# Two gated MLPs: second products by Strassen's scheme on token halves, with weight sums on GpSimd

## The chip, the cores and the metric

One core of a Trainium2 chip runs the whole program. The metric is the device time of one execution in microseconds, the median of the runs shown. The engines are TensorE (PE; its weight loads are listed apart as PEld), VectorE (DVE), ScalarE (ACT), GpSimd (POOL) and SyncE (SP), which issues most DMAs.

## The reference, cut to what matters

Batch 1, 512 tokens, width 1024, all in float32. Five other stages lie around two gated MLPs (an S5 mixer, two attention stages, a Mamba-2 layer and norms). The change touches only the MLPs, with 2816 hidden channels:

```
def conv_ffn(xn, w_up, conv_w, conv_b, w_down):
    val, gate = jnp.split(xn @ w_up, 2, axis=-1)
    gp = jnp.pad(gate, ((0, 0), (CONV_W - 1, 0), (0, 0)))
    gc = conv_b + conv_w[0] * gp[:, 0:seq]
    for j in range(1, CONV_W):
        gc = gc + conv_w[j] * gp[:, j:j + seq]
    return (jax.nn.silu(gc) * val) @ w_down
...
h = h + conv_ffn(rms_norm(h, ffn_norm[layer]), ffn_w_up[layer], ...)
```

`xn @ w_up` is the first product, `(...) @ w_down` the second one.

## The kernel before, in words

Channels lie on the 128 partitions, the 512 tokens on the free axis. The state `K.h` is 8 tiles of 128x512; the hidden activations of an MLP are 22 tiles. Every dense product is made in three passes of reduced-precision matmuls: weight and activation are each split into a high part (rounded to fp32r) and the remainder, and high*high, high*low and low*high are added up in one PSUM bank (`product`, lines 431, 432, 434). The remainder times remainder is dropped.

Weights come from device memory in *units*, in the order of one list (`weight_units`). A unit of an MLP's first product is 8 blocks of 128 columns (1024 columns of float32, 512 KB). An output of the second product sums over 11 hidden tiles in each half of the MLP, cut into a unit of 6 blocks and one of 5. For each unit SP issues a load into one of 5 buffers `raw` (`weight_loads`), ACT rounds it into one of 3 buffers `wh` (`split_hi`, line 391), DVE subtracts and writes `wl` (`split_lo`, line 402), and PE counts the unit as done. So the high part of unit n waits until PE is done with unit n-3, and the load of unit n+5 waits for both parts of unit n. ACT and DVE execute in the order of the code: `split_hi(K, act, upto)` and `split_lo(K, dve, upto)` are placed between the other work, two units (`LA`) ahead of PE.

`ffn_pe`, `ffn_act`, `ffn_dve` and `ffn_pool` are one MLP. A half is an *up* stretch, then a *down* stretch. In an up stretch PE makes for each hidden tile f the gate and the value (two units, 48 matmuls of 512 columns). For each f DVE multiplies the gate with the norm's factors (line 705), makes the convolution (802, 805, 808) and one `wl`, waits for ACT's SiLU (771), multiplies by the norm (812) and the value (815); ACT rounds the result into `fh` (776), DVE writes the remainder `fl` (819), and then makes the other `wl`. In a down stretch PE makes the 8 output tiles, and DVE adds each to `h` (719). In the second half ACT and DVE also make the next stage's input from each finished `h` tile (`norm_act`: 542, 562; `norm_dve`: 550), and GpSimd sums the squares (577). GpSimd has nothing else to do in the MLPs.

Of the kernel before, what the change touches and what calls it, by code (L numbers as in the profile page):

```python
# [8 lines left out]
P = 128  # L9
# [4 lines left out]
HALF = NF // 2  # L14
# [16 lines left out]
RAW, NH, LA = 5, 3, 2  # L31

# [211 lines left out]
def weight_units():  # L244

    u = []

    def tile(name, m, k0=0, k1=8):
        for a, z in pieces(k0, k1):
            u.append((name, "T", m, a, z))  # L250

    def tiles(name, ms):
        for m in ms:
            tile(name, m)

    def values(name):
        for half in range(2):
            for k in range(0, 8, 2):
                u.append((name, "N", D + half * 512, k, k + 2))

    def ffn(i):
        tiles(f"up{i}", (NF, 0))
        for half in range(2):
            for f in range(half * HALF, (half + 1) * HALF):
                if f:
                    tiles(f"up{i}", (NF + f, f))
            for m in range(8):
                tile(f"down{i}", m, half * HALF, (half + 1) * HALF)
# [34 lines left out]
WIDTH = {"T": P, "N": 512, "N32": 32}  # L303
# [3 lines left out]
OFFS = [P * sum(COLS[:n]) for n in range(len(UNITS) + 1)]  # L307


def done(name, m, k0=0, k1=8):  # L310

    return UNIT[(name, "T", m, pieces(k0, k1)[-1][0])] + 1

# [20 lines left out]
    + ["gcp", "conv", "silu", "gv", "fh", "fl"]  # L334
# [6 lines left out]
    + ["lam", "lama", "akc", "aqc", "ag", "agg", "agt", "asp", "asc", "aex", "acm", "atp", "akp", "amix"]  # L341
# [399 lines left out]
def ffn_pe(K, pe, layer):  # L741
# [15 lines left out]


def ffn_act(K, act, layer):
# [4 lines left out]
    for half in range(2):  # L764
        for f in range(half * HALF, (half + 1) * HALF):
# [5 lines left out]
            act.e.activation(t[:, :], t[:, :], ACT.Silu).then_inc(K.S["silu"], 1)  # L771
# [5 lines left out]
        for m in range(8):  # L777
            split_hi(K, act, done(down, m, half * HALF, (half + 1) * HALF) + LA)
            if half:
                norm_act(K, act, b + 1, m)  # L780


def ffn_dve(K, dve, layer):
# [8 lines left out]
    for half in range(2):  # L792
        for f in range(half * HALF, (half + 1) * HALF):
# [17 lines left out]
            dve.wait_ge("silu", i + 1)  # L811
# [2040 lines left out]
def combine2_dve(K, dve, n):  # L2852
# [3 lines left out]
    dve.wait_ge("lam", 4)  # L2856
# [169 lines left out]
def att2_dve(K, dve):  # L3026
# [197 lines left out]
def att1_tensors(K, sb):  # L3224
# [11 lines left out]
    K.sp = [[(sb("sph0", [P, 1024], R32), sb("spl0", [P, 1024], R32)), (K.wh[0], K.wl[0])],  # L3236
# [56 lines left out]
def build_program(nc, d):  # L3293
    with ExitStack() as ctx:
# [18 lines left out]
        K.xs = [sb(f"xs{i}", [P, T]) for i in range(2)]  # L3313
# [126 lines left out]
def _weights(inputs):  # L3440
# [8 lines left out]
    for n, (name, kind, m, k0, k1) in enumerate(UNITS):  # L3449
        c0, cw = (m * P, P) if kind == "T" else (m, WIDTH[kind])  # L3450
# [26 lines left out]
```

## Time and profile before

| | us |
|---|---|
| time, median of 3 runs (1982.88 to 1983.55) | 1983.34 |
| span of the profiled execution, first to last instruction | 1981.3 |
| what lies around the span (1983.34 - 1981.3) | 2.0 |
| PE busy in the span | 1953.9 |
| DVE, ACT, POOL busy | 1329.3, 900.1, 243.7 |
| first MLP: up 258.4 to 367.3, down to 427.1, up to 546.8, down to 606.6 | 348 |
| second MLP: up 895.1 to 1003.9, down to 1063.8, up to 1183.4, down to 1243.2 | 348 |

The execution that was profiled has no time of its own beside its span; the span and the median differ by 2.0 us. A span entry for PE counts overlapping matmuls once. The columns of each view are explained at its first group of rows below.

### The profile page before, as it was taken

The numbers are of one execution on the slowest core, as the hardware profiler recorded it, in microseconds if no ns is written. First come the engines' busy times: TensorE is split into PE (matmuls) and PEld (weight loads), VectorE is DVE, ScalarE is ACT, GpSimd is POOL, SyncE is SP. The second block draws the span as 40 slices with busy tenths as digits, with TensorE's granted clock in tenths as the row PEclk, the third lists the DMA queues.
The fourth block names the chain that finished last, engine by engine and source line by source line (L and its number), as shares of the span: only waits on it lengthen the run. The fifth ranks groups of instructions, "written<-read, shape, count | busy, mean of one in ns | idle before, by whom it ended". The sixth has DMA issues, their size and how long they took to land.

```text
span 1981.3 us, 25092 instructions
## 1 busy us (share of the span) xinstructions
PE 1953.9 (99%) x9474; PEld 1562.3 (79%) x9474; DVE 1329.3 (67%) x1907; ACT 900.1 (45%) x1483; POOL 243.7 (12%) x237
## 2 busy tenths in 40 slices
PE   9999999999999999999999999999999999999998
PEld 7777888888888776788888888788888888886666
DVE  8995476446644449747644664778787778437985
ACT  5674332223233348733222223565555545236774
POOL 4131100000010000010000001133333332000002
PEclk9999999999999999999999999999999999999998
DMA  8465322232233220022223223222222223322112
GB/s 290 113 144 155 106 83 92 88 121 91 81 105 106 86 96 11 1 90 91 93 88 117 96 77 107 86 64 70 86 75 80 85 65 107 96 75 75 38 38 75
DMA packets 81367, 180.44 MB, mean 91 GB/s; under 512 B 17888, under 2 KB 33632, under 8 KB 81248
## 3 DMA queue, kind: packets, MB, share of 16 engines
q1 hardware_dynamic: 77680, 172.08, 27.9%
q0 software_dynamic: 3424, 6.23, 1.1%
q8 instruction: 76, 1.25, 0.3%
q10 hardware_dynamic: 144, 0.52, 0.1%
q14 instruction: 43, 0.35, 0.1%
HBM read 171.53 MB, written 7.27 MB: 90 GB/s over the span
## 4 chain that ended last, share of the span: by engine, by line
PE 85%; DVE 8%; ACT 3%; issue 2%; DMA 1%; SPq 1%; POOLq 0%; POOL 0%; DVEq 0%; ACTq 0%
PE psum L431 20%; PE psum L434 20%; PE psum L432 20%; PE psum L472 2%; PE psum L473 2%; PE psum L475 2%; PE psum L453 2%; PE psum L899 1%; PE psum L901 1%; PE psum L900 1%; PE psum L1781 1%; PE psum L456 1%; PE psum L454 1%; PE psum L2824 1%; DVE wl L402 1%
## 5 line engine op out<-in xcount | busy, mean ns | idle before, releaser
L402 DVE TENSOR_TENSOR wl<-raw,wh 128x1024 fp32r<-128x1024 f32 (+3 forms) x337 | 381.4, 1133 | 303.6 <-ACT wh L391 302.9
L431 PE MATMUL psum<-xh,wh 128*128 128x512 f32 x1376 | 543.9, 395 | 1.7 <-DVE xl L550 1.7
L434 PE MATMUL psum<-xh,wl 128*128 128x512 f32 x1376 | 537.0, 390 | 1.6 <-DVE wl L402 1.6
L432 PE MATMUL psum<-xl,wh 128*128 128x512 f32 x1376 | 536.4, 390 | 0.0
L391 ACT ACTIVATE wh<-raw 128x1024 fp32r<-128x1024 f32 (+3 forms) x337 | 316.0, 939 | 294.8 <-PE psum L434 198.1
L431 PEld LDWEIGHTS psum<-xh,wh 128*128 128x128 f32 x1376 | 258.6, 188 | 61.9 <-issue 2.9
L434 PEld LDWEIGHTS psum<-xh,wl 128*128 128x128 f32 x1376 | 258.7, 188 | 57.9 <-DVE wl L402 3.7
L432 PEld LDWEIGHTS psum<-xl,wh 128*128 128x128 f32 x1376 | 258.8, 188 | 55.1 <-issue 2.4
L577 POOL TENSOR_TENSOR rs<-rs,sq 128x512 f32<-128x512 f32 x35 | 46.6, 1331 | 1088.8 <-ACT sq L562 1088.8
L434 PE MATMUL psum<-fh,wl 128*128 128x512 f32 x352 | 136.9, 389 | 0.0
L432 PE MATMUL psum<-fl,wh 128*128 128x512 f32 x352 | 136.9, 389 | 0.0
L431 PE MATMUL psum<-fh,wh 128*128 128x512 f32 x352 | 136.9, 389 | 0.0
L719 DVE TENSOR_TENSOR h<-h,psum 128x512 f32<-128x512 f32 x87 | 59.3, 684 | 67.7 <-PE psum L434 65.4
L431 PEld LDWEIGHTS psum<-fh,wh 128*128 128x128 f32 x352 | 66.1, 188 | 13.8
L434 PEld LDWEIGHTS psum<-fh,wl 128*128 128x128 f32 x352 | 66.1, 188 | 13.7
L432 PEld LDWEIGHTS psum<-fl,wh 128*128 128x128 f32 x352 | 66.1, 188 | 13.6
L542 ACT ACTIVATE xh<-h,par 128x512 fp32r<-128x512 f32 x64 | 43.5, 715 | 63.8 <-DVE h L719 55.2
L771 ACT ACTIVATE ny<-ny 128x512 f32<-128x512 f32 x22 | 13.9, 632 | 109.6 <-DVE ny L808 109.6
L771 ACT ACTIVATE nv<-nv 128x512 f32<-128x512 f32 x22 | 13.9, 632 | 104.0 <-DVE nv L808 104.0
L472 PE MATMUL psum<-xh,wh 128*128 128x512 f32 x152 | 59.6, 392 | 0.4 <-ACT xh L1382 0.4
L475 PE MATMUL psum<-xh,wl 128*128 128x512 f32 x152 | 59.2, 390 | 0.0
L473 PE MATMUL psum<-xl,wh 128*128 128x512 f32 x152 | 59.2, 390 | 0.0
(526 smaller groups left out, 3339.1 us busy)
## 6 DMA issues: line engine op xcount, KB each, us to landing
raw<-d_w SPq DMA_DIRECT2D x224, 512.0 KB, 3.5
raw<-d_w SPq DMA_DIRECT2D x32, 384.0 KB, 3.0
raw<-d_w SPq DMA_DIRECT2D x48, 256.0 KB, 2.6
raw<-d_w SPq DMA_DIRECT2D x32, 320.0 KB, 2.9
Mt<-d_kd SPq DMA_DIRECT2D x64, 64.0 KB, 2.4
bc<-d_bc SPq DMA_DIRECT2D x8, 256.0 KB, 5.3
d_ud<-ust SPq DMA_DIRECT2D x8, 256.0 KB, 3.1
U<-d_ud POOLq DMA_DIRECT2D x64, 32.0 KB, 2.4
```

The costliest lines, as they stand in the source:

```text
L391: act.e.activation(K.wh[n % NH][:, 0:COLS[n]], K.raw[n % RAW][:, 0:COLS[n]], ACT.Copy).then_inc(K.S["hi"], 1)
L402: dve.e.tensor_tensor(K.wl[n % NH][:, 0:COLS[n]], K.raw[n % RAW][:, 0:COLS[n]], K.wh[n % NH][:, 0:COLS[n]].bitcast(F32), ALU.subtract).the ...
L431: pe.e.matmul(b[:, :], WH[:, o:o + P], XH, start=(k == k0), stop=False)
L432: pe.e.matmul(b[:, :], WH[:, o:o + P], XL, start=False, stop=False)
L434: mm = pe.e.matmul(b[:, :], WL[:, o:o + P], XH, start=False, stop=(k == k1 - 1))
L453: pe.e.matmul(b[:, :], WH[:, o:o + P], XH, start=(k == 0), stop=False)
L472: pe.e.matmul(b[:, :], WH[:, o:o + P], XH, start=(k == 0), stop=False)
L473: pe.e.matmul(b[:, :], WH[:, o:o + P], XL, start=False, stop=False)
L475: mm = pe.e.matmul(b[:, :], WL[:, o:o + P], XH, start=False, stop=(k == 7))
L542: act.e.activation(K.xh[:, k, :], K.h[:, k, :], ACT.Copy, scale=K.par(gain, k)).then_inc(K.S["xh"], 1)
L577: pool.e.tensor_tensor(K.acc[:, :], K.acc[:, :], K.sq[k % 2][:, :], ALU.add).then_inc(K.S["acc"], 1)
L719: dve.e.tensor_tensor(K.h[:, m, :], K.h[:, m, :], K.bank[bank][:, :], ALU.add).then_inc(K.S[signal], 1)
```

## The change

The second product now takes hidden tiles in pairs (k, k+1), outputs in pairs q and tokens in halves L and R of 256. In such a 2x2 by 2x2 product the weights are the blocks A11, A12, A21, A22 and the activations B11, B12 (first hidden tile, L and R), B21, B22. Strassen's scheme in Winograd's form makes it with seven products of 256 columns instead of eight. It needs four sums of the weights (S1 to S4) and four of the activations (T1 to T4), and recombines the products.

- The MLP is cut into 12 and 10 hidden tiles instead of 11 and 11 (`SPANS`). In the first half all 8 outputs go by the scheme (4 pairs), in the second 6 outputs (3 pairs); outputs 6 and 7 of the second half are made by `product` as before.
- A unit "S" holds 4 blocks for one pair of outputs and one of hidden tiles: 256 KB are loaded, GpSimd appends three more blocks of sums (`weight_sums`), and ACT and DVE split the 7 blocks, 896 columns. `split_hi` waits for GpSimd's count `wsum`.
- PE makes 7 x 3 matmuls of 256 columns for a unit, into four banks (`seven_products`).
- For an odd hidden tile, DVE makes T2, T3, T4 and the remainders of 512 and of 1024 columns; for an even one T1 and a remainder of 256 (first half) or 512 columns (`hidden_dve`). T1 to T4 lie in `K.T`, named `xs` in the rows.
- A pair of outputs is added to `h` by eight instructions of DVE and a copy of one product out of PSUM by ACT (`seven_to_h`).
- GpSimd makes all weight sums of an MLP before it adds the first squares (`ffn_pool`). The spare buffers that the first attention borrows, and the counts of a few semaphores, are renamed.

```diff
-HALF = NF // 2
+SPANS = ((0, 12), (12, NF))
+DOWN_PAIRS = (4, 3)
...
+def weight_sums(K, pool, name):
+    for n, u in enumerate(UNITS):
+        if u[:2] != (name, "S"):
+            continue
...
+        pool.wait_ge(f"raw{n % RAW}", 16 * (n // RAW + 1))
+        pool.e.tensor_tensor(s13.rearrange("p (n c) -> p n c", n=2), a21.unsqueeze(1).broadcast_to([P, 2, P]),
+                             others.rearrange("p (n c) -> p n c", n=2), ALU.add).then_inc(K.S["pool"], pool.up())
+        pool.wait_ge("pool", pool.n)
+        pool.e.tensor_tensor(s2, s1, a11, ALU.add).then_inc(K.S["pool"], pool.up())
+        pool.wait_ge("pool", pool.n)
+        pool.e.tensor_tensor(s4, s2, a12, ALU.add).then_inc(K.S["wsum"], 1)
...
+A22, A11, A12, S1, S3, S2, S4 = range(7)
+SEVEN = ((A11, "B11", 0, 0), (A12, "B21", 2, 0), (S4, "B22", 2, 1), (A22, "T4", 3, 0), (S1, "T1", 3, 1), (S2, "T2", 0, 1),
+         (S3, "T3", 1, 0))
+def seven_products(K, pe, name, q, banks, x, freed, k0, k1):
...
+    for k in range(k0, k1, 2):
+        n, WH, WL = next_unit(K, pe, name, "S", q, k)
+        pe.wait_ge("hi", n + 1)
...
+            pe.e.matmul(out, WH[:, o:o + P], XH, start=first, stop=False, skip_group_check=True)
+            pe.e.matmul(out, WH[:, o:o + P], XL, start=False, stop=False, skip_group_check=True)
+            pe.wait_ge("lo", n + 1)
+            mm = pe.e.matmul(out, WL[:, o:o + P], XH, start=False, stop=(k == k1 - 2), skip_group_check=True)
+        mm.then_inc(K.S["unit"], 1)
...
+def seven_to_h(K, dve, q, banks, end, copy, before, signal):
...
+    split_lo(K, dve, end + 1 + LA)
+    dve.wait_ge(*before)
+    dve.wait_ge("unit", end)
+    a = add(h1, h1, p23[:, :], ALU.add)
+    dve.wait_ge("fa", copy)
+    u = add(U, p16[:, R], p1, ALU.subtract)
+    dve.wait_ge("dve", a)
+    add(h1[:, L], h1[:, L], p1, ALU.add)
+    dve.wait_ge("dve", u)
+    w = add(Q, U, p7[:, L], ALU.subtract)
+    split_lo(K, dve, end + 2 + LA)
+    b = add(h1[:, R], h1[:, R], U, ALU.subtract)
+    c = add(h2, h2, p45[:, :], ALU.add)
+    dve.wait_ge("dve", b)
+    e.tensor_tensor(h1[:, R], h1[:, R], p45[:, R], ALU.subtract).then_inc(K.S[signal], 1)
+    dve.wait_ge("dve", max(w, c))
+    two = h2.rearrange("p (n c) -> p n c", n=2)
+    e.tensor_tensor(two, two, Q.unsqueeze(1).broadcast_to([P, 2, 256]), ALU.add).then_inc(K.S[signal], 1)
...
             split_hi(K, act, v + 1 + LA)
-            if f >= 13:
-                act.wait_ge("unit", done(down, 7, 0, HALF))
-            act.wait_ge("gv", i + 1)
-            act.e.activation(K.fh[layer][:, f % 13, :], t[:, :], ACT.Copy).then_inc(K.S["fh"], 1)
...
+            act.wait_ge("gv", val_read(i))
+            if f % 2 == 0:
+                n = 1 + half
+                act.e.activation(hidden(K.fh[layer], half, f, "B11", n), t[:, 0:256 * n], ACT.Copy).then_inc(K.S["fh"], 1)
+            else:
+                act.e.activation(hidden(K.fh[layer], half, f, "B21", 2), t[:, :], ACT.Copy).then_inc(K.S["fh"], 1)
+                act.wait_ge("gv", val_read(i) + 1)
+                act.e.activation(hidden(K.fh[layer], half, f, "T1", 4), K.T[:, :], ACT.Copy).then_inc(K.S["fh"], 1)
...
 def ffn_pool(K, pool, layer):
+    weight_sums(K, pool, f"down{layer}")
     add_squares(K, pool, 2 + 2 * layer)
```

The order of DVE's instructions at the end of the first up stretch of the first MLP (the last hidden tile, then the first units of the second product). Before, with the last tile's gate at the top (`psum,rs`), `wl` of 768 and 640 columns for the second product, and `h<-h,psum` for the first output:

```order
L705 TENSOR_TENSOR fg_1<-psum,rs 128x512
L802 TENSOR_SCALAR nv<-fg_1,par 128x512
L805 SCALAR_TENSOR_TENSOR nv<-fg_1,par,nv 128x511
L808 SCALAR_TENSOR_TENSOR nv<-fg_1,par,nv 128x510
L402 TENSOR_TENSOR wl<-raw,wh 128x640
L812 TENSOR_TENSOR nv<-nv,rs 128x512
L815 TENSOR_TENSOR nv<-nv,psum 128x512
L819 TENSOR_TENSOR fl<-nv,fh 128x512
L402 TENSOR_TENSOR wl<-raw,wh 128x768
L402 TENSOR_TENSOR wl<-raw,wh 128x640
L719 TENSOR_TENSOR h<-h,psum 128x512
```

And now, from the convolution's last instruction of hidden tile 11 (an odd one) to the first pair of outputs; `xs` is `K.T`:

```order
L990 SCALAR_TENSOR_TENSOR ny<-fg_2,par,ny 128x510
L418 TENSOR_TENSOR wl<-raw,wh 128x896
L994 TENSOR_TENSOR ny<-ny,rs 128x512
L997 TENSOR_TENSOR ny<-ny,psum 128x512
L955 TENSOR_TENSOR xs<-ny,xs 128x256
L956 TENSOR_TENSOR xs<-ny,nv 128x256
L958 TENSOR_TENSOR xs<-ny,xs 128x256
L961 TENSOR_TENSOR fl<-ny,fh 128x512
L961 TENSOR_TENSOR fl<-xs,fh 128x1024
L418 TENSOR_TENSOR wl<-raw,wh 128x896 x7
L475 TENSOR_TENSOR h<-h,psum 128x512
```

Between the last multiplication by the value and the next `wl` there are now five instructions of DVE instead of one.

ACT's order around the end of the first pair of outputs in the second half, now (`wh<-raw` are the splits, `xs<-psum` the copy of one product, `xh`, `rs` and `sq` the next stage's input and its squares):

```order
L406 ACTIVATE wh<-raw 128x896 x6
L927 ACTIVATE xs<-psum 128x256
L406 ACTIVATE wh<-raw 128x896
L633 ACTIVATE xh<-h,par 128x512
L650 ACTIVATE rs<-h 128x512
L633 ACTIVATE xh<-h,par 128x512
L653 ACTIVATE sq<-h 128x512
L406 ACTIVATE wh<-raw 128x896 x4
```

Two `h` tiles become ready together, so four activations stand between two splits, where before there were two for every two splits.

## Rows read from the trace of the kernel before

**Rows 1.** The page: span, and each engine's busy time and share.

```profile
span 1981.3 us, 25092 instructions
...
PE 1953.9 (99%) x9474; PEld 1562.3 (79%) x9474; DVE 1329.3 (67%) x1907; ACT 900.1 (45%) x1483; POOL 243.7 (12%) x237
```

**Rows 2.** Windows of MLP 1, second to fourth stretch: us, busy (instructions), clock, DMA.

```profile
367.30:427.10 59.80, 59.80 (x265) 49.53 (x264) 21.54 (x26) 13.77 (x17) 0.00 (x0) 1.00 0.36 113
427.10:546.80 119.70, 119.70 (x530) 99.12 (x529) 77.14 (x98) 33.75 (x43) 0.00 (x0) 1.00 0.28 89
546.80:606.60 59.80, 59.80 (x265) 49.55 (x264) 28.07 (x32) 21.69 (x31) 7.77 (x6) 1.00 0.36 113
```

**Rows 3.** Timeline, PE in attention 1: start, duration, line, tiles.

```profile
753.30 0.28 PE L1064 MATMUL psum<-spl,tri 128*128 128x256 f32 x1
...
753.77 0.40 PE L1069 MATMUL psum<-sph,tri 128*128 128x512 f32 x1
```

**Rows 4.** The same, 12 us later.

```profile
765.18 0.28 PE L1064 MATMUL psum<-spl,tri 128*128 128x256 f32 x1
...
765.54 0.28 PE L1068 MATMUL psum<-wh,tri 128*128 128x256 f32 x1
```

**Rows 5.** Timeline, DVE, a hidden tile of the up stretch.

```profile
351.22 0.69 DVE L705 TENSOR_TENSOR fg<-psum,rs 128x512 f32<-128x512 f32 x1 [0.96 <-PE psum L434]
...
353.31 0.75 DVE L808 SCALAR_TENSOR_TENSOR ny<-fg,par,ny 128x510 f32<-128x510 f32 x1
355.71 1.23 DVE L402 TENSOR_TENSOR wl<-raw,wh 128x1024 fp32r<-128x1024 f32 x1 [1.65 <-ACT wh L391]
...
357.58 0.69 DVE L815 TENSOR_TENSOR ny<-ny,psum 128x512 f32<-128x512 f32 x1
358.96 0.69 DVE L819 TENSOR_TENSOR fl<-ny,fh 128x512 fp32r<-128x512 f32 x1 [0.70 <-ACT fh L776]
```

**Rows 6.** Timeline, ACT, the same tile: SiLU and rounding into fh.

```profile
354.10 0.63 ACT L771 ACTIVATE ny<-ny 128x512 f32<-128x512 f32 x1 [5.10 <-DVE ny L808]
...
358.30 0.63 ACT L776 ACTIVATE fh<-ny 128x512 fp32r<-128x512 f32 x1 [2.62 <-DVE ny L815]
```

**Rows 7.** Timeline, DVE, gate of hidden tile 1 of MLP 1.

```profile
269.31 0.68 DVE L705 TENSOR_TENSOR fg<-psum,rs 128x512 f32<-128x512 f32 x1
```

**Rows 8.** Timeline, PE: the first weights' remainder that came late.

```profile
275.07 0.50 PE L434 MATMUL psum<-xh,wl 128*128 128x512 f32 x1 [0.46 <-DVE wl L402]
```

**Rows 9.** Groups by form, DVE: count, busy us, mean ns, idle before.

```profile
L1713 DVE TENSOR_TENSOR mst<-mst,sq 128x256 f32<-128x256 f32 x16 | 6.8, 425 | 15.6 <-ACT mst L1705 15.3
```

**Rows 10.** The same, ACT.

```profile
L391 ACT ACTIVATE wh<-raw 128x1024 fp32r<-128x1024 f32 x224 | 235.2, 1052 | 152.4 <-PE psum L434 58.0 <-PE psum L901 50.0 <-PE psum L475 36.1
...
L391 ACT ACTIVATE wh<-raw 128x256 fp32r<-128x256 f32 x1 | 0.4, 417 | 0.0
```

**Rows 11.** The same, POOL.

```profile
L577 POOL TENSOR_TENSOR rs<-rs,sq 128x512 f32<-128x512 f32 x35 | 46.6, 1331 | 1088.8 <-ACT sq L562 1088.8
...
L2244 POOL TENSOR_TENSOR s5small<-s5small 128x64 f32<-128x64 f32 x1 | 0.3, 328 | 0.1
```

**Rows 12.** Timeline, POOL, second down stretch of MLP 1.

```profile
571.54 1.29 POOL L577 TENSOR_TENSOR rs<-rs,sq 128x512 f32<-128x512 f32 x1 [6.18 <-ACT sq L562]
```

**Rows 13.** Timeline, DVE, the same place.

```profile
572.23 1.42 DVE L402 TENSOR_TENSOR wl<-raw,wh 128x768 fp32r<-128x768 f32 x1 [1.39 <-ACT wh L391]
...
576.98 0.69 DVE L719 TENSOR_TENSOR h<-h,psum 128x512 f32<-128x512 f32 x1 [1.81 <-PE psum L434]
```

**Rows 14.** Timeline, DVE, first down stretch: a remainder of 768 columns.

```profile
369.86 0.96 DVE L402 TENSOR_TENSOR wl<-raw,wh 128x768 fp32r<-128x768 f32 x1
```

**Rows 15.** Timeline, ACT, second down stretch: the next stage's input.

```profile
577.70 0.72 ACT L542 ACTIVATE xh<-h,par 128x512 fp32r<-128x512 f32 x1 [3.39 <-DVE h L719]
578.33 0.62 ACT L562 ACTIVATE sq<-h 128x512 f32<-128x512 f32 x1
```

**Rows 16.** DMA issues: count, KB each, median us to landing.

```profile
raw<-d_w SPq DMA_DIRECT2D x48, 256.0 KB, 2.6
```

More of the change, by code:

```diff
@@ L262, in ffn @@
         tiles(f"up{i}", (NF, 0))
-        for half in range(2):
-            for f in range(half * HALF, (half + 1) * HALF):
+        for half, (f0, f1) in enumerate(SPANS):
+            for f in range(f0, f1):
                 if f:
                     tiles(f"up{i}", (NF + f, f))
-            for m in range(8):
-                tile(f"down{i}", m, half * HALF, (half + 1) * HALF)
+            for q in range(DOWN_PAIRS[half]):
+                for k in range(f0, f1, 2):
+                    u.append((f"down{i}", "S", q, k, k + 2))
+            for m in range(2 * DOWN_PAIRS[half], 8):
+                tile(f"down{i}", m, f0, f1)
     tiles("a_w_in", range(8))
@@ L307, with pair_done @@
 OFFS = [P * sum(COLS[:n]) for n in range(len(UNITS) + 1)]
+SUMS = [sum(u[1] == "S" for u in UNITS[:n + 1]) for n in range(len(UNITS))]
+SPLIT = [(P, 7 * P) if u[1] == "S" else (0, c) for u, c in zip(UNITS, COLS)]
 def done(name, m, k0=0, k1=8):
     return UNIT[(name, "T", m, pieces(k0, k1)[-1][0])] + 1
+def pair_done(name, q, k1):
+    return UNIT[(name, "S", q, k1 - 2)] + 1
 SEMS = (
@@ L763, in ffn_act @@
     rsqrt_first(K, act, b)
-    for half in range(2):
-        for f in range(half * HALF, (half + 1) * HALF):
+    for half, (f0, f1) in enumerate(SPANS):
+        for f in range(f0, f1):
             i = layer * NF + f
@@ L770, in ffn_act @@
             act.other("silu")
[L771 removed]
+            act.e.activation(t[:, :], t[:, :], ACT.Silu).then_inc(K.S["fa"], 1)
             split_hi(K, act, v + 1 + LA)
[L773 to L780 removed]
+            if half:
+                act.wait_ge("unit", pair_done(down, 3, SPANS[0][1]))
@@ new lines, in ffn_act @@
+        for q in range(DOWN_PAIRS[half]):
+            for k in range(f0, f1, 2):
+                split_hi(K, act, UNIT[(down, "S", q, k)] + 1 + LA)
+            end = pair_done(down, q, f1)
+            split_hi(K, act, end + 1 + LA)
+            act.wait_ge("unit", end)
+            act.wait_ge("fl", 33 * layer + 3 * (f1 // 2))
+            if q:
+                act.wait_ge("h" if half else "hpart", (8 + 16 * layer if half else 8 * layer) + 2 * q)
+            act.e.activation(K.T[:, 512:768], K.bank[DOWN_BANKS[half][q % 2][0]][:, 0:256], ACT.Copy).then_inc(K.S["fa"], 1)
+            split_hi(K, act, end + 2 + LA)
+            if half:
+                norm_act(K, act, b + 1, 2 * q)
+                norm_act(K, act, b + 1, 2 * q + 1)
@@ new lines, in ffn_act, with hidden_dve @@
+        for m in range(2 * DOWN_PAIRS[half], 8):
+            split_hi(K, act, done(down, m, f0, f1) + LA)
+            norm_act(K, act, b + 1, m)
+def hidden_dve(K, dve, layer, half, f):
+    i, e = layer * NF + f, dve.e
+    t, before, g = K.gg[i % 2], K.gg[(i + 1) % 2], 33 * layer + 3 * (f // 2)
+    L, R = slice(0, 256), slice(256, 512)
+    T1, T2, T3, T4 = (K.T[:, 256 * n:256 * n + 256] for n in range(4))
+    if half:
+        dve.wait_ge("unit", pair_done(f"down{layer}", 3, SPANS[0][1]))
+    dve.wait_ge("gv", val_read(i))
+    if f % 2 == 0:
+        n = 1 + half
+        dve.wait_ge("fl", g)
+        own(K, dve, "dve", e.tensor_tensor(T1, t[:, R], t[:, L], ALU.subtract))
+        dve.wait_ge("fh", g + 1)
+        e.tensor_tensor(hidden(K.fl[layer], half, f, "B11", n), t[:, 0:256 * n],
+                        hidden(K.fh[layer], half, f, "B11", n).bitcast(F32), ALU.subtract).then_inc(K.S["fl"], 1)
+        return
+    e.tensor_tensor(T2, t[:, R], T1, ALU.subtract).then_inc(K.S["dve"], dve.up())
+    e.tensor_tensor(T3, t[:, R], before[:, R], ALU.subtract).then_inc(K.S["dve"], dve.up())
+    dve.wait_ge("dve", dve.n)
+    e.tensor_tensor(T4, t[:, L], T2, ALU.subtract).then_inc(K.S["gv"], 1)
+    for first, n, count, src in (("B21", 2, g + 2, t[:, :]), ("T1", 4, g + 3, K.T[:, :])):
+        dve.wait_ge("fh", count)
+        e.tensor_tensor(hidden(K.fl[layer], half, f, first, n), src, hidden(K.fh[layer], half, f, first, n).bitcast(F32),
+                        ALU.subtract).then_inc(K.S["fl"], 1)
@@ L791, in ffn_dve @@
     newton(K, dve, K.ny[:, :], K.nv[:, :], K.ns[:, :], K.rs[:, :]).then_inc(K.S["rs"], 1)
-    for half in range(2):
-        for f in range(half * HALF, (half + 1) * HALF):
+    for half, (f0, f1) in enumerate(SPANS):
+        for f in range(f0, f1):
             i = layer * NF + f
```

142 lines of the change are left out of this document (98 added, 44 removed).

## The prediction

> **What bounds the kernel now.** I read the page first: PE is busy for 1953.9 of 1981.3 us, DVE for 67%, ACT for 45%, GpSimd for 12% [rows 1]. Then the windows of the first MLP. In the down stretches PE has no gap (59.80 busy of 59.80), DVE is busy for 21.5 or 28 us, ACT for 14 or 22, at a granted clock of 1.00 [rows 2]. So matmul time saved here is saved on the path, as long as DVE and ACT, which prepare every operand, stay ahead. The up stretches have less room than their shares say: a hidden tile gives PE 48 matmuls, and DVE and ACT work on it in turns, each waiting for the other. Therefore I then read the timeline of one such tile, tile by tile.
>
> **PE: what is removed and added.** A down stretch has 8 x 11 x 3 = 264 matmuls of 512 columns in 59.80 us, 0.2265 us each [rows 2]. One MLP has 528, 119.6 us. After: 4 pairs of outputs x 6 pairs of hidden tiles + 3 x 5 = 39 units of 21 matmuls, 819 of 256 columns, and 2 x 10 x 3 = 60 of 512. The nearest rows for 256 columns with a new weight tile each are those of attention 1: four starts in 753.77 - 753.30 = 0.47 us, 0.117 each [rows 3], and three in 0.36 us, 0.120 each [rows 4]. I take 0.119: 819 x 0.119 + 60 x 0.2265 = 97.5 + 13.6 = 111.1 us, 8.5 less for an MLP, 17.1 for both. At 0.120 it is 15.4, at 0.117 it is 20.4. Against the one eighth of the work that is dropped, some is lost since 256 columns take more than half the time of 512.
>
> The Trainium skill (TensorE: Matmul & The Clock Gate, "Back-to-back issue gap") gives N/2.4 + 2.5 ns at full clock, 216 ns for 512 columns and 109 for 256. By that an MLP would save 528 x 0.216 - 819 x 0.109 - 60 x 0.216 = 11.8 us, both 23.7. The rows (226.5 and 117 to 120) do not agree, and they decide.
>
> **The up stretch.** In the rows of one tile, from the start of L705: L808 2.09, ACT's SiLU 2.88, the first remainder L402 4.49, L815 6.36, ACT's fh 7.08, fl 7.74 [rows 5, 6]. fh is followed by ACT's split of 1.05 us [rows 10] and the second remainder of 1.23; the next L705 could start at 9.83. PE takes 48 x 0.2268 = 10.89 us, so before DVE gains 1.06 us for each tile when it is behind. Now an odd tile goes: L815 ends at 7.05, three instructions of 256 columns (0.425 each [rows 9], the first two overlapped by 0.09) to 8.27, ACT rounds 1024 columns to 9.36, DVE's remainder ends at 10.62, the second wl at 11.75, next L705 at 11.66. For an even tile the 256-column rounding (0.417 [rows 10]) gives 9.62 in the first half, and 512 columns 9.83 in the second. A pair takes 21.28 or 21.49 of PE's 21.77 us. PE isn't delayed in the stretch itself (a remainder has some 4.5 us to spare), but a lag of DVE is hardly made good any more.
>
> The lag at the start is known: L705 of tile 1 comes at 269.31 [rows 7]; 19 units of 5.44 us back from 367.3 [rows 2], less 0.5 for a wait of PE, put the end of its gate at 263.4, so that it is 5.8 us late; it costs PE about 0.5 us in tile 2 [rows 8]. Now it starts at about 5.3 (tile 0 has smaller roundings), PE loses about the same, and it falls by 0.49 a pair from 4.0 at tile 3 to 1.85 at tile 11 (0.24 of it since the units there have 896 columns). The second up stretch starts with DVE 4.0 us late, because `seven_to_h` of the last pair holds DVE until 9.8 us after PE's start, where the wait is for a unit of 5.44 us; but there tile 12 misses its first wl and SiLU's split, 2.1 us, so that the lag is 0.9 at tile 13 and about 0 at the end.
>
> **From up to down.** Let PE begin the first S unit at V. It takes two units, 2 x 21 x 0.119 = 5.0 us, and needs the remainder of the third at V + 5.24. A wl of 896 columns takes (0.96 + 1.23)/2 = 1.09 us [rows 14, 5], ACT's split 0.93 [rows 10]. DVE reaches L815 at V + 0.95 + lag and, by the steps above, ends that remainder 5.26 later: V + 6.2 + lag. Before, a unit had 3.4 or 4.1 us of PE and only one fl, and nothing was late. So PE now waits 1.0 us + lag: 2.85 us in the first half, 1.0 in the second, before GpSimd is counted.
>
> **GpSimd.** 128x512 took 1.29 us undisturbed [rows 12], 128x64 0.33 [rows 11], so 2.15 ns a column: 0.74 us for 256 columns, 0.46 for each 128, 1.67 and two short waits for a unit, below PE's 2.50. A unit's load lands 2.6 us after its issue [rows 16], which follows the wl five units ahead; the sums are ready some 5 us before ACT needs them. But GpSimd and DVE exclude each other: the addition from 571.54 to 572.83 made the remainder that started at 572.23 last 1.42 us instead of 0.96 [rows 12 to 14], that is until 0.82 us after GpSimd was through, as if it had started just before that end. Instructions that read PSUM, such as L719, are not stretched. GpSimd's hold of a unit is at most 1.67 - 3 x 0.14 = 1.24 us. I laid the seven sums that fall into tiles 8 to 11 (each lands 2.7 us after a wl) against DVE's steps. Every second one falls into the wait for SiLU and costs nothing; the others push DVE by 0.54, 0.27, 0.24 and 0.27. That is 1.3 us in the first half, and 0.5 in the second, where the lag's reserve takes the rest. Bounds: none, and 7 x 1.24 = 8.7 us for a transition. I take the sums' values, since they rest on the same steps. PE waits 4.2 and 1.5 us, 5.7 for an MLP.
>
> The Trainium skill (GPSIMD Engine Reference, "Specifications" and "Engine selection") says that GpSimd shares its SBUF port with VectorE, with contention where a DVE instruction has two SBUF inputs, and that elementwise work belongs on VectorE, about twice as fast. The trace agrees on the contention (1.42 against 0.96 us) and with 1.29 against 0.69 us. This rule speaks against the change; its result is the second rival below.
>
> **End of a pair of outputs.** After PE's last matmul of a pair ACT splits (0.93) and copies, and DVE does wl, four additions, wl, four additions. The eight cost 3 x 0.69 [rows 13] + 5 x 0.425 = 4.2 us, against 2 x 0.69 before. In the first half the wl after them ends at 8 us after the pair, and PE wants it at 4 x 2.50 + 0.24 = 10.24: no wait. In the second half ACT waits for h at 6.1 and makes xh, sq, xh, sq (0.72, 0.62 [rows 15]) to 8.6; its split ends at 9.4, DVE's wl at 10.55: PE waits 0.35 us. For the second pair GpSimd's sum of squares (1.29) lies before the wl, which ends at 11.45: 1.25 us. The third pair is followed by units of 3.4 us and hides it. Queued behind ACT's wait for h are all splits. 1.6 us for an MLP. Nothing changes after output 7.
>
> **The sum.** Profiled span 1981.3 + 2.0 around it = 1983.3, the median. 1983.3 - 17.1 + 2 x (5.7 + 1.6) = 1983.3 - 17.1 + 14.6 = 1980.8 us.
>
> **Rivals.**
> First, DVE's lag disappears: the sums all fall into waits and the first up stretch ends without lag. For it speaks that PE waits for a remainder only at tile 2 before, and that half of DVE's steps are waits for ACT; against it the 0.49 us a pair, which cannot repay 4 us. PE would wait 1.0 at each transition and 0.35 twice: 2.7 for an MLP. 1983.3 - 17.1 + 5.4 = 1971.6.
> Second, and slower: GpSimd's hold decides at the transitions. Three separate additions with waits between them may each catch a DVE instruction; with half the full hold, 0.62 us a unit, seven units push DVE by 4.3 instead of 1.3 and, in the second half, 3.5 instead of 0.5. That adds 3.0 us at four transitions, 12: 1992.8. It decides from (1987.3 - 1980.8)/4 = 1.6 us more at a transition, 0.4 us a unit in the mean. For it: DVE wants the port for half of a tile's time. Against: a wait for ACT after every second step lets it catch up.
> Third, 256-column matmuls are bound by their weight loads at 0.120 or a little more in a long row, with every PE number else as above: 0.123 would take 6.6 us of the gain, 1987.4. Rows 3 and 4 are short rows of four, which speaks for a doubt; their starts stay at 0.12, which speaks against.
>
> **How the numbers follow.** The forecast's case has 0.42, the first rival 0.24, the second 0.24, the third 0.10. A measurement of this kernel tells about 0.2% (4 us) from no change, so faster is below 1979.4, slower above 1987.3. The forecast's own range, with transitions off by 1 us each, is 1976 to 1986: 0.15 of its 0.42 is faster, 0.26 same, 0.01 slower. The first rival is faster. The second is slower but for 0.02. The third is same or slower in equal parts. Sum: faster 0.39, same 0.33, slower 0.28. The range reaches from 1969 (first rival, with 0.117 for a matmul) to 1995 (second rival, somewhat beyond its mean); outside lies a tenth on either side.
>
> **What would show it.** Starts 0.119 apart in the units of 256 columns and down stretches near 24 x 2.50 + 4.2 = 64 us (first half) and 15 x 2.50 + 13.6 + 1.5 + 1.6 = 54 us (second). A wait of PE for wl in the third S unit of each down stretch, about 4 and 1.5 us, and small ones in the fifth unit of pairs 1 and 2 in the second half; none in the first half's pairs. L705 of tile 11 about 3 us behind its gate, and of tile 21 under 1. Additions of GpSimd of 0.46 to 0.74 us, longer where they meet DVE. I am wrong in the mechanism if PE waits elsewhere, such as for ACT's high part or for `wsum`, or if the up stretches grow by more than 1 us each.

## The result and the profile after

The changed kernel takes 1994.13 us (median of 4 runs, 1993.26 to 1995.15), the kernel before on the same chip 1983.44 (1982.88 to 1984.29): a ratio of 1.0053 [1.0038, 1.0067]. It is slower by half a per cent; the forecast was 1980.8. The page of the profiled execution, for [rows 1]:

```profile
span 1992.5 us, 27125 instructions
...
PE 1946.9 (98%) x10176; PEld 1587.2 (80%) x10176; DVE 1465.0 (74%) x2123; ACT 952.9 (48%) x1541; POOL 438.9 (22%) x471
```

The span grew by 11.2 us, and PE's busy time fell by 7.0, so PE stands still for 18.2 us more (what lies between its records). DVE is busy for 136 us more, GpSimd for 195. Which stretches changed is read from windows: us, busy (instructions) of PE, PEld, DVE, ACT, POOL, then the granted clock, DMA share and GB/s. The first three lines are the stretches of the first MLP that [rows 2] show of before, the next two the down stretches of the second MLP; the last is a piece of the first line.

```profile
378.12:445.85 67.73, 63.95 (x505) 63.16 (x504) 47.56 (x58) 26.75 (x31) 45.52 (x57) 0.95 0.38 115
445.85:554.68 108.83, 108.83 (x483) 90.09 (x481) 83.26 (x116) 35.45 (x44) 13.19 (x18) 1.00 0.28 85
554.68:612.58 57.90, 52.76 (x377) 49.37 (x375) 45.02 (x58) 27.21 (x39) 33.03 (x34) 1.00 0.37 110
1021.37:1087.91 66.54, 62.72 (x505) 62.11 (x504) 46.87 (x58) 26.76 (x31) 47.13 (x57) 0.97 0.39 117
1196.74:1254.79 58.05, 52.81 (x377) 49.38 (x375) 45.03 (x58) 27.39 (x39) 33.24 (x34) 1.00 0.35 103
...
388.10:393.60 5.50, 5.50 (x26) 5.50 (x27) 2.21 (x3) 0.95 (x1) 2.79 (x6) 0.50 0.46 143
```

The up stretch is unchanged: its window now holds ten tiles, 10.88 us each, as PE's 48 x 0.2268. The four down stretches took 59.8 us each; now they sum to 250.2 instead of 239.2. That is all but 0.2 us of the loss. In two of them the clock is below 1.00, where [rows 2] have 1.00.

PE, in the steady part of a down stretch (start, duration, line, tiles), for [rows 3, 4]:

```profile
400.01 0.28 PE L462 MATMUL psum<-fh,wl 128*128 128x256 f32 x1
400.13 0.28 PE L459 MATMUL psum<-fh,wh 128*128 128x256 f32 x1
```

Starts lie 0.120 apart. The Trainium skill (TensorE: Matmul & The Clock Gate, "Back-to-back issue gap") has a formula for an isolated matmul that gives 0.109; this trace does not agree.

The second S unit of the first down stretch (its wait is at 381.89) and the third one (386.39 and 388.07), PE:

```profile
381.89 0.39 PE L462 MATMUL psum<-fh,wl 128*128 128x256 f32 x1 [0.62 <-DVE wl L418]
...
386.39 0.38 PE L459 MATMUL psum<-fh,wh 128*128 128x256 f32 x1 [1.97 <-ACT wh L406]
386.61 0.28 PE L460 MATMUL psum<-fl,wh 128*128 128x256 f32 x1
388.07 0.58 PE L462 MATMUL psum<-fh,wl 128*128 128x256 f32 x1 [1.18 <-DVE wl L418]
388.45 0.42 PE L459 MATMUL psum<-fh,wh 128*128 128x256 f32 x1
388.67 0.41 PE L460 MATMUL psum<-fl,wh 128*128 128x256 f32 x1
```

PE waits three times in 6.2 us, and behind the last wait the starts go from 0.12 to 0.21 apart: TensorE is at 1.2 instead of 2.4 GHz (0.50 in the window 388.10 to 393.60). It had stood still for 2.0 and 1.2 us just before. 25 matmuls here and 16 in the second MLP start 0.213 apart, 41 x 0.093 = 3.8 us. What DVE and ACT did meanwhile, for [rows 5 to 7]:

```profile
374.86 1.58 DVE L418 TENSOR_TENSOR wl<-raw,wh 128x896 fp32r<-128x896 f32 x1 [0.34 <-ACT wh L406]
376.37 0.68 DVE L796 TENSOR_TENSOR fg<-psum,rs 128x512 f32<-128x512 f32 x1
...
380.74 1.09 DVE L418 TENSOR_TENSOR wl<-raw,wh 128x896 fp32r<-128x896 f32 x1 [1.54 <-ACT wh L406]
...
383.98 0.43 DVE L958 TENSOR_TENSOR xs<-ny,xs 128x256 f32<-128x256 f32 x1
...
386.67 3.61 DVE L418 TENSOR_TENSOR wl<-raw,wh 128x896 fp32r<-128x896 f32 x3
```

```profile
384.44 1.06 ACT L917 ACTIVATE fh<-xs 128x1024 fp32r<-128x1024 f32 x1 [0.62 <-DVE xs L958]
385.40 2.61 ACT L406 ACTIVATE wh<-raw 128x896 fp32r<-128x896 f32 x3
```

The third S unit's high part is the first of the three at 385.40. It stands behind the rounding of T1 to T4 on ACT, which waits for T4 (L958). Its remainder, the first of three from 386.67, is what PE waits for until 388.07. And the last gate of the stretch (L796) was itself late. The additions of GpSimd around it, for [rows 12]:

```profile
374.76 0.73 POOL L431 TENSOR_TENSOR raw<-raw 128x256 f32<-128x256 f32 x1 [1.63 <-DMA raw<-d_w]
375.58 1.19 POOL L434 TENSOR_TENSOR raw<-raw 128x128 f32<-128x128 f32 x1
376.84 0.46 POOL L436 TENSOR_TENSOR raw<-raw 128x128 f32<-128x128 f32 x1
```

The remainder from 374.86 took 1.58 us where 1.09 is usual (380.74), and GpSimd's addition of 128 columns beside it 1.19 where 0.46 is usual (376.84). Each held the other up: the addition of 256 columns that was under way until 375.49 held up the remainder, and the remainder held up the next addition. Lastly PE's waits grouped (engine, line, what it waited for, us in total, times, longest):

```profile
PE psum L462 <- DVE wl L418: 11.8, 10, 1.7
PE psum L459 <- ACT wh L406: 6.2, 6, 2.0
```

By stretch, measured by what they add to a down stretch without waits (60.47 and 51.42 us, from the last experiment but one) and without the clock's share: the first down stretches wait 5.0 and 4.6 us, the second ones 6.5 and 6.6, of which 2.4 and 2.5 lie at their start and 4.1 and 4.1 behind pairs 1 and 2. The account of the 11.2 us: matmuls -15.4, waits +22.7, clock +3.8, in all 11.1. The 22.7 are more than the 18.2 us of standing still because a wait adds more than the gap between two records: the record before it lasts 0.28 us where the next start would have come after 0.12, and the first start behind it is followed by the next after 0.22 (386.39 to 386.61).

### The profile page after: what moved, and what is told of

It reads as the page before. It is cut to its first block, busy times and chain, and to the rows that moved or that the text cites. A ratio compares the mean times of both kernels' runs of the same rounds, so it can differ in the third digit from the quotient of the medians.

```text
span 1992.5 us, 27125 instructions
## 1 busy us (share of the span) xinstructions
PE 1946.9 (98%) x10176; PEld 1587.2 (80%) x10176; DVE 1465.0 (74%) x2123; ACT 952.9 (48%) x1541; POOL 438.9 (22%) x471
## 4 chain that ended last, share of the span: by engine, by line
PE 63%; DVE 21%; ACT 8%; issue 7%; DMA 1%; SPq 0%; DVEq 0%; ACTq 0%
PE psum L522 10%; PE psum L525 10%; PE psum L523 10%; ACT wh L406 4%; DVE wl L418 3%; PE psum L462 3%; PE psum L459 3%; PE psum L460 3%; PE psum L563 2%; PE psum L566 2%; PE psum L564 2%; PE psum L544 1%; PE psum L1084 1%; PE psum L1085 1%; PE psum L1086 1%
## 5 line engine op out<-in xcount | busy, mean ns | idle before, releaser
L418 DVE TENSOR_TENSOR wl<-raw,wh 128x1024 fp32r<-128x1024 f32 (+3 forms) x359 | 427.9, 1197 | 280.0 <-ACT wh L406 279.4
L525 PE MATMUL psum<-xh,wl 128*128 128x512 f32 x1376 | 537.6, 391 | 1.7 <-DVE wl L418 1.7
L523 PE MATMUL psum<-xl,wh 128*128 128x512 f32 x1376 | 536.3, 390 | 0.0
L431 POOL TENSOR_TENSOR raw<-raw 128x256 f32<-128x256 f32 x78 | 71.1, 911 | 468.6 <-DMA raw<-d_w 468.5
L462 PE MATMUL psum<-fh,wl 128*128 128x256 f32 x546 | 157.4, 288 | 11.8 <-DVE wl L418 11.8
L459 PE MATMUL psum<-fh,wh 128*128 128x256 f32 x546 | 157.2, 288 | 6.2 <-ACT wh L406 6.2
L460 PE MATMUL psum<-fl,wh 128*128 128x256 f32 x546 | 156.1, 286 | 0.0
L462 PEld LDWEIGHTS psum<-fh,wl 128*128 128x128 f32 x546 | 106.6, 195 | 13.8 <-DVE wl L418 13.8
L459 PEld LDWEIGHTS psum<-fh,wh 128*128 128x128 f32 x546 | 106.7, 195 | 7.8 <-ACT wh L406 7.6
L434 POOL TENSOR_TENSOR raw<-raw 128x128 f32<-128x128 f32 x78 | 62.9, 806 | 6.1
L436 POOL TENSOR_TENSOR raw<-raw 128x128 f32<-128x128 f32 x78 | 58.9, 755 | 6.1
```

Source lines behind the costliest of these rows:

```text
L418: dve.e.tensor_tensor(K.wl[n % NH][:, 0:w], K.raw[n % RAW][:, o:o + w], K.wh[n % NH][:, 0:w].bitcast(F32), ALU.subtract).then_inc(K.S["lo" ...
L431: pool.e.tensor_tensor(s13.rearrange("p (n c) -> p n c", n=2), a21.unsqueeze(1).broadcast_to([P, 2, P]), others.rearrange("p (n c) -> p n ...
L434: pool.e.tensor_tensor(s2, s1, a11, ALU.add).then_inc(K.S["pool"], pool.up())
L436: pool.e.tensor_tensor(s4, s2, a12, ALU.add).then_inc(K.S["wsum"], 1)
L459: pe.e.matmul(out, WH[:, o:o + P], XH, start=first, stop=False, skip_group_check=True)
L460: pe.e.matmul(out, WH[:, o:o + P], XL, start=False, stop=False, skip_group_check=True)
```

## The experiments

Theory A, the prediction's with larger sizes: the splits of the next units queue behind the serial chain of the last hidden tile and behind the pair's additions; GpSimd's hold of the port lengthens that chain; the clock falls when PE has waited. B: GpSimd's additions are the whole cause. C: they hardly matter. The kernel before took 1983.39 us beside the first four and 1983.19 beside the last four. Lines with < are taken out of the changed kernel, those with > put in.

**No sums.** GpSimd's additions are left out, so the weights' products use unsummed blocks.

```diff
<         if UNITS[n][1] == "S":
<             act.wait_ge("wsum", SUMS[n])
...
<     weight_sums(K, pool, f"down{layer}")
```

> GpSimd's weight sums are left out (ACT and DVE split whatever lies in the three blocks of the sums), so nothing shares the SBUF port with DVE in the MLPs but the sums of squares. Theory A (the waits come from the chain that DVE and ACT walk in turns, now longer by T1 to T4, by the eight instructions for a pair and by the splits queued behind them; GpSimd only lengthens it): PE's waits in the two MLPs fall from 22.5 to about 9 to 11 us, the clock stays up (another 4), 1976 to 1980 us. Theory B (GpSimd's hold on the port is what makes DVE late): hardly a wait is left, 1967 to 1970 us. Theory C (port contention matters little): within 4 us of 1994.

Measured 1982.59 us (10 runs), ratio 0.9996 [0.9986, 1.0005]: 11.5 less than with the sums. A's number is missed by some 3 us, B's by 13, and C's (no more than 4 us) is excluded. Windows:

```profile
378.20:443.13 64.93, 62.48 (x505) 62.07 (x504) 41.41 (x56) 26.30 (x31) 0.00 (x0) 0.97 0.42 119
551.96:606.78 54.82, 52.19 (x376) 49.23 (x375) 40.53 (x58) 27.35 (x38) 9.75 (x6) 1.00 0.38 116
1015.62:1079.06 63.44, 60.98 (x505) 60.57 (x504) 41.41 (x56) 26.32 (x31) 0.00 (x0) 1.00 0.42 123
```

```profile
374.88 0.68 DVE L793 TENSOR_TENSOR fg<-psum,rs 128x512 f32<-128x512 f32 x1
```

Without the weight sums the first down stretch still waits 3.0 us, by the chain alone, and the second 3.4, with GpSimd's sums of squares still beside it (9.75 us in its window). The gate of tile 11 comes 3.32 us before the stretch, with the sums 1.75. The clock fell once (0.97, 15 matmuls), in the first MLP; the second MLP's first down stretch has waits of the same size and stayed at 1.00. So the sums cost some 9.7 us of waits and 2.5 of clock, more than twice what had been counted, and they aren't the whole cause.

**No T.** T1 to T4, their rounding and remainder are cut to 8 columns; PE reads blocks of the plain hidden tile in their place.

```diff
>         block = {"T1": "B11", "T2": "B21", "T3": "B22", "T4": "B11"}.get(block, block)
...
<     T1, T2, T3, T4 = (K.T[:, 256 * n:256 * n + 256] for n in range(4))
---
>     T1, T2, T3, T4 = (K.T[:, 256 * n:256 * n + 8] for n in range(4))
```

> T1 to T4 and their splits are cut to 8 columns, and PE multiplies B blocks in their place; all counts, waits and matmuls stay. Theory A: DVE has no lag at the end of the up stretches, the waits at the first units of the second product (4.9 and 2.4 us for an MLP) and the fallen clock go, those at the ends of pairs stay: 1976 to 1979 us. Theory B: the port is held as before, so at least half of the waits at the first units stay, 1984 to 1990 us.

Measured 1976.67 (5 runs), 0.9966 [0.9953, 0.9979]: what A had, and far from B's.

```profile
377.41:437.99 60.58, 60.58 (x505) 60.52 (x504) 44.91 (x56) 24.45 (x29) 45.90 (x54) 1.00 0.43 128
546.82:602.54 55.72, 52.44 (x377) 49.31 (x375) 43.33 (x58) 26.28 (x38) 32.23 (x33) 1.00 0.38 114
```

With the sums in place and the tile's chain shorter no wait is left at the start of a down stretch, and the clock stays at 1.00. Only the waits behind pairs remain, 4.3 us in the second stretch. The hold alone makes nothing late at the start of a down stretch.

**Plain addition.** A pair is added with two instructions of 512 columns, so h isn't the combination wanted.

```diff
<     u = add(U, p16[:, R], p1, ALU.subtract)
...
<     add(h1[:, L], h1[:, L], p1, ALU.add)
...
<     w = add(Q, U, p7[:, L], ALU.subtract)
>     e.tensor_tensor(h1, h1, p23[:, :], ALU.add).then_inc(K.S[signal], 1)
...
>     e.tensor_tensor(h2, h2, p45[:, :], ALU.add).then_inc(K.S[signal], 1)
```

> A pair of outputs is added to h by two instructions of 512 columns instead of eight (six are left out; ACT's copy stays). Theory A: the waits at the ends of pairs in the second half (4.2 us for an MLP) go and nothing else changes: 1985 to 1987 us. Theory B: GpSimd's additions before the late wl stay, so 1 to 2 us of each MLP's 4.2 stay: 1988 to 1990 us.

Measured 1986.14 (10 runs), 1.0013 [1.0003, 1.0022], 8.0 less than the changed kernel, as A had it.

```profile
553.98:607.28 53.30, 51.94 (x377) 49.17 (x376) 37.48 (x40) 27.48 (x38) 31.17 (x33) 1.00 0.40 119
```

The waits behind the pairs are gone, those at the start (1.9 us here, 6.4 with the clock in the first stretch) aren't. To leave six of a pair's eight additions out is thus enough to remove the 8.2 us that stood there, with the weight sums in place. That it is also possible without leaving anything out is shown by the run "Pair early" below.

**Units early.** In the last tile of each up stretch the third and fourth S units are split before the norm's multiplication, the fifth before ACT rounds T1 to T4.

```diff
>             if f == f1 - 1:
>                 split_hi(K, act, v + 5)
...
>     if f == SPANS[half][1] - 1:
>         split_lo(K, dve, done(f"up{layer}", NF + f) + 6)
...
<             split_lo(K, dve, done(up, NF + f) + 1 + LA)
---
>             split_lo(K, dve, done(up, NF + f) + 1 + LA + 2 * (f == f1 - 1))
```

> Nothing is left out; in the last hidden tile of each up stretch ACT and DVE split the third and fourth unit of the second product right after the second, before the norm's multiplication, and the fifth before the rounding of T1 to T4. Theory A (the order of the splits behind the tile's own steps is what makes PE wait): the waits of 4.9 and 2.4 us for an MLP and the fallen clock go, 1975 to 1978 us. Theory B (DVE has too little time in all, with GpSimd on its port): the wait only moves to a later unit or to the tile's remainder, 1988 to 1994 us.

Measured 1987.24 (10 runs), 1.0018 [1.0008, 1.0027]; A had 1975 to 1978 and missed by 9 us; it is just under B's 1988 to 1994.

```profile
378.32:440.13 61.81, 61.04 (x505) 60.62 (x504) 47.75 (x58) 26.64 (x31) 48.01 (x57) 1.00 0.42 125
548.96:608.08 59.12, 53.97 (x376) 50.81 (x375) 46.07 (x58) 27.25 (x39) 31.90 (x34) 0.97 0.36 108
...
562.00:566.00 4.00, 4.00 (x25) 4.00 (x24) 2.23 (x2) 0.66 (x1) 2.92 (x3) 0.63 0.42 98
```

```profile
561.58 0.36 PE L459 MATMUL psum<-fh,wh 128*128 128x256 f32 x1 [2.38 <-DVE fl L967]
```

The first down stretch gets 5.9 us shorter, the second 1.2 longer. There PE sums over five pairs of tiles, so it wants tile 21 itself in its fifth unit, not its sixth. One unit too many had been put ahead of the tile: the wait moved from the weights to `fl`. That is what B had said for the second halves; that it is the number of units put ahead, and not too little time in all, is shown by the run "Both early". The clock fell right behind this wait in the first MLP, for some 15 matmuls. In the second MLP the wait for `fl` (2.1 us at 1199.58) was followed by no fall, and the clock fell only behind pair 2, after a wait of 1.7 us.

**Pair early.** In the second half the fifth unit after pairs 1 and 2 is split before the next stage's xh, sq and xl.

```diff
>                 if q < 2:
>                     split_hi(K, act, end + 3 + LA)
...
>                 if q < 2:
>                     split_lo(K, dve, pair_done(down, q, f1) + 3 + LA)
```

> Nothing is left out; in the second halves, after pairs 1 and 2, ACT and DVE split the fifth unit of the next pair before they make the next stage's input from h, instead of after. Theory A (the splits queued behind ACT's wait for h are what PE waits for at the ends of pairs): 4.2 us of waits for an MLP go, 1985 to 1987 us, as when six of the eight instructions are left out. Theory B (the port is full there, so the wait moves elsewhere): at least half stays, 1989 to 1993 us.

Measured 1988.68 (7 runs), 1.0026 [1.0015, 1.0037], 5.4 less than the changed kernel.

```profile
380.30:448.23 67.93, 64.06 (x506) 63.26 (x505) 47.30 (x58) 26.76 (x31) 45.48 (x57) 0.95 0.40 115
557.05:611.54 54.49, 52.20 (x376) 49.09 (x375) 45.96 (x58) 27.74 (x39) 34.74 (x35) 1.00 0.39 117
1020.35:1085.00 64.65, 61.24 (x506) 60.62 (x504) 47.74 (x57) 26.75 (x31) 47.80 (x57) 1.00 0.41 117
1193.83:1249.43 55.60, 53.43 (x376) 50.67 (x375) 45.22 (x58) 27.93 (x39) 33.11 (x35) 0.97 0.36 107
```

The waits behind the pairs go without a single instruction less: their order made them. A's 1985 to 1987 is missed by 2 us, and B's 1989 to 1993 by less. In part the waits moved, as B had it: those at the start of the second down stretches are 3.1 and 2.9 us instead of 2.4 and 2.5. The rest of the miss can't be read off as one term, because the clock fell at other places than in the changed kernel: once more in the second MLP's second down stretch (0.97, some 1.3 us), and once ahead of the MLPs (0.62 from 174.0 to 178.5, behind a wait of 2.2 us; the first down stretch begins 2.2 us later), but not in the second MLP's first down stretch, which is 1.9 us shorter than in the changed kernel (64.65 for 66.54) at the same two waits of 2.0 and 1.2 us.

**Both early.** The two before together, one unit fewer ahead in the second half.

```diff
>                 split_hi(K, act, v + 5 - half)
...
>         split_lo(K, dve, done(f"up{layer}", NF + f) + 6 - half)
...
>             split_lo(K, dve, done(up, NF + f) + 1 + LA + (2 - half) * (f == f1 - 1))
```

> Nothing is left out; both orders together, and in the second up stretch one unit less is taken ahead than in the run before, where the third unit ahead pushed the remainder fl past its need. Theory A: the waits add up, so do the gains: 1983.4 - 15.4 of PE's time + 2 to 4 us of waits = 1970 to 1972 us, faster than the kernel before. Theory B (too little time in all for DVE next to GpSimd): 1978 us or more.

Measured 1971.92 (4 runs, 1971.20 to 1973.11), 0.9942 [0.9927, 0.9957]: faster than both kernels, 22.2 us less than the changed one, and A's 1970 to 1972.

```profile
378.11:439.94 61.83, 60.96 (x505) 60.56 (x504) 47.83 (x58) 26.63 (x31) 48.10 (x57) 1.00 0.40 123
548.77:600.73 51.96, 51.68 (x376) 49.06 (x375) 47.30 (x58) 27.77 (x39) 35.65 (x34) 1.00 0.41 122
```

```profile
380.50 3.29 DVE L418 TENSOR_TENSOR wl<-raw,wh 128x896 fp32r<-128x896 f32 x3 [1.54 <-ACT wh L406]
383.71 0.68 DVE L1002 TENSOR_TENSOR ny<-ny,rs 128x512 f32<-128x512 f32 x1
```

DVE now does three remainders, those of the second to fourth unit, while the rest of tile 11 waits. The last of them ends at 383.79, where in the changed kernel PE waited for the third unit's until 388.07, and tile 11 itself is wanted only in the sixth unit. The DVE and GpSimd work is the same, and in this profile the clock falls in none of the four down stretches.

**Both early, no sums.** The same without GpSimd's additions.

```diff
<     weight_sums(K, pool, f"down{layer}")
```

> The two orders as before, and GpSimd's weight sums left out (whatever lies in their blocks is split). Theory A: the port costs 1 to 3 us at most once the splits come early: 1968 to 1970 us. Theory B: 8 us or more below the same kernel with the sums.

Measured 1968.93 (4 runs), 0.9926 [0.9911, 0.9941], as A had it.

```profile
378.29:438.77 60.48, 60.48 (x506) 60.47 (x505) 41.32 (x56) 26.19 (x31) 0.00 (x0) 1.00 0.44 128
547.59:599.01 51.42, 51.42 (x376) 49.06 (x375) 41.43 (x58) 27.55 (x38) 9.69 (x6) 1.00 0.41 124
```

PE has no gap: this is the floor, 504 x 0.120 = 60.5 and 315 x 0.120 + 13.6 = 51.4 us. The same additions that cost 11.5 us behind the late splits cost 3.0 here.

**Filler.** Five float32 matmuls of constants in front of the third S unit of the first down stretch, so that PE doesn't stand still there.

```diff
>         if k0 == 0 and q == 0 and k == 4:
>             pe.wait_ge(*pe.freed[0])
>             for _ in range(5):
>                 pe.e.matmul(K.bank[0][:, :], K.con("ones"), K.con("alibi"), start=True, stop=True)
```

> The changed kernel with five matmuls of 512 float32 columns (0.43 us each, 2.2 in all) into a free bank, where PE otherwise stands still for 2.1 us before the third unit of the first down stretch of each MLP. If the fallen clock there comes from PE standing still (theory A), it stays up and 3 to 4 us are saved: 1990 to 1991 us. If the clock falls for another reason, or still falls since PE also waits before and after, 1993 to 1995 us.

Measured 1993.92 (4 runs), 1.0052 [1.0036, 1.0069]: A's 1990 to 1991 is missed.

```profile
383.79 4.45 PE L454 MATMUL psum<-con 128*128 128x512 f32 x10
```

```profile
388.20:393.20 5.00, 5.00 (x44) 5.00 (x43) 2.92 (x3) 0.95 (x1) 2.67 (x4) 1.00 0.54 160
...
560.70:564.00 3.30, 3.30 (x18) 3.30 (x18) 1.21 (x2) 0.72 (x1) 1.37 (x3) 0.53 0.83 225
```

The place where the clock had been 0.50 is at 1.00 in both MLPs. That fits the idea that PE's standing still lets it fall there, but it is one profile, and the second MLP of "Pair early" has the same waits, no filler and no fall either, so it is not shown. The five matmuls ran as ten records that start 0.43 us apart, 4.3 us in all instead of 2.2, so the first down stretches gained only 2.1 and 1.2 us (65.66 and 65.31). In the first MLP's second down stretch the clock now fell twice (0.53 in the second window), where the changed kernel had kept it. The whole time is unchanged. Why it fell there, behind waits of the same size as in the changed kernel, stays open.

## Why the prediction was wrong

The sum was 1983.3 - 17.1 + 14.6 = 1980.8. Measured it is 1983.3 - 15.4 + 22.7 + 3.8 = 1994.4, for 1994.1. The time lies in the range, in the wrong direction; it is near the second rival's 1992.8, though neither place nor size of that rival's 12 us is what happened. Point by point:

- **Matmuls**: 0.120 and not 0.119, which [rows 4] had and [rows 3] had not. The gain is 15.4. Small, and settled by the floor.
- **Up stretch**: right. No loss there, and the lag of 1.85 us (how late DVE is) at tile 11 is what the kernel without sums shows: its last gate is started 3.32 us before the end of the stretch, and with no lag it would be 5.17 (a unit of 5.44 less 0.27 of PE's own delay). With the sums it is 5.17 - 1.75 = 3.4 us, where about 3 was forecast.
- **From up to down, without the weight sums**: right in size. 2.85 and 1.0 were predicted; without sums 3.0 and 1.1 were measured. That PE would wait in the third unit alone was wrong (it also waited in the second, for the remainder that DVE began at 380.74), and so was that it would wait for the remainder alone: of the 5 us two were for ACT's high part, which the prediction had named as a sign that the mechanism is wrong. It is the same chain, since both parts stand behind T4, and the delay is shared between them.
- **GpSimd: the step that failed.** The hold of its weight sums was priced at 1.3 and 0.5 us for the two transitions of an MLP and at nothing behind the pairs. Measured, as the waits with sums less those without: 1.8, 1.3, and 1.8 behind the two pairs, 4.9 an MLP against 1.8; more than half of the difference lies behind the pairs. At the transitions I laid each sum against DVE's steps as if its place were known. At the pairs I didn't lay it at all, though the sums run there too. After pair 1 in the second stretch, DVE and GpSimd:

```profile
573.43 0.41 DVE L475 TENSOR_TENSOR xs<-xs,psum 128x256 f32<-128x256 f32 x1
...
574.76 0.68 DVE L475 TENSOR_TENSOR h<-h,xs 128x256 f32<-128x256 f32 x1
...
579.65 4.20 DVE L418 TENSOR_TENSOR wl<-raw,wh 128x896 fp32r<-128x896 f32 x3 [1.67 <-ACT wh L406]
...
589.74 0.41 DVE L475 TENSOR_TENSOR h<-h,xs 128x256 f32<-128x256 f32 x1
```

```profile
573.30 0.53 POOL L434 TENSOR_TENSOR raw<-raw 128x128 f32<-128x128 f32 x1
573.91 1.25 POOL L436 TENSOR_TENSOR raw<-raw 128x128 f32<-128x128 f32 x1
...
579.64 0.74 POOL L431 TENSOR_TENSOR raw<-raw 128x256 f32<-128x256 f32 x1
580.45 1.18 POOL L434 TENSOR_TENSOR raw<-raw 128x128 f32<-128x128 f32 x1
```

  The addition with both inputs outside PSUM took 0.68 beside GpSimd, and 0.41 without it (589.74, after pair 2); the one that reads PSUM took 0.41 beside GpSimd too (573.43). Three remainders took 4.20 us, against 3 x 1.09 = 3.3 alone; and PE waited for the first of them, the fifth unit's (1.2 us at 581.38). Behind pair 2 the long wait (1.7 us at 596.58) is beside GpSimd's sum of squares, which was counted, and which is there without the weight sums too.
- **End of a pair, without the weight sums**: 2.3 us against 1.6, the order of size that was forecast.
- **Clock: a second step that failed, a term put at nothing.** The prediction's "granted clock of 1.00" was read from stretches without waits [rows 2] and carried over to ones with waits. Measured: 3.8 us, 41 matmuls at 1.2 GHz.
- **First rival** (all sums fall into waits): excluded, since taking them out gave 11.5 us. **Second**: its hold of 3.0 us more at each of four transitions is not there; measured it is 0.5 and 0.8 more. **Third**: its 0.123 is excluded, the starts lie 0.120 apart.

Of the 13.6 us missed, GpSimd's hold is 9.8 - 3.6 = 6.2, the clock 3.8, the chain and the pairs without the weight sums 12.9 - 11.0 = 1.9, and the matmuls 1.7. All but the matmuls' share depends on the order: the same instructions in another one are 11.3 us faster than the kernel before.

## What to carry to other kernels

When an engine's work in front of a transition grows, look at what the next stage wants first and move its operands' preparation ahead of the serial chain, but never so far that the chain's own result becomes the late one; that order was worth 22 us here where the additions' removal was worth 11.5. Price a wait of PE with the clock that it may cost, and price an engine that shares the port where the other is behind, not by its mean: the same additions cost 3.0 us under early splits and 11.5 under late ones.

## What the runs showed of the hardware

- The exclusion of GpSimd and DVE works both ways. An addition of 128 columns on GpSimd took 0.46 us alone and up to 1.40 beside a remainder of DVE; DVE's remainder of 896 columns 1.09 alone and up to 1.67 beside GpSimd's weight sums, in the changed kernel. The Trainium skill (SBUF — State Buffer, "Who interferes with whom") has an exclusive lock where the loser blocks; the trace agrees (0.73 us more for GpSimd, 0.49 for DVE).
- PE's clock fell to 1.2 GHz behind two waits of 2.0 and 1.2 us, and 256-column matmuls then started 0.213 apart. The size of the waits alone doesn't decide it: behind the same 2.0 and 1.2 us it fell in the first MLP of "Pair early" and not in the second. Waits of 0.4 and 1.7 us (594.38 and 596.58 in the changed kernel) were followed by no fall; the filler's kernel has waits of 0.4 and 1.7 us at the same place and a fall right behind. What decides is not settled by these runs.
- A float32 matmul of 512 columns with constants ran as two records that start 0.43 us apart at full clock.
